# An encoder block on one core: high and low parts of Q and K made in the projection, 64-row third score product, attention's first tiles among the projection's last groups

## What is computed

```python
proj = rmsnorm(h) @ w_in            # 2048 x 2048: q 512, k 512, v 512, u 512
# per head (4), two score maps c=0,1 of depth 64 share one value matrix of width 128
sc = einsum('bqhcd,bkhcd->bhcqk', q, k) * 64**-0.5
p  = softmax(sc - slope_h * |qpos - kpos|)
att = (p[c=0] - lam * p[c=1]) @ v   # lam from four vectors of 64
ssm = bi_s5_glu(u)                  # two-way state-space scan and gate
h = h + concat(rmsnorm(att), ssm) @ w_out
y = rmsnorm(h + relu(rmsnorm(h) @ w_mlp1)**2 @ w_mlp2)
```

## Time and profile before

| | us |
|---|---|
| median of three runs | 2686.13 |
| the three runs | 2683.91, 2686.13, 2692.33 |
| span of the profiled execution | 2681.7 |
| TensorE busy | 2562.9 (96%) |
| VectorE busy | 2093.3 (78%) |
| ScalarE busy | 1416.5 (53%) |
| POOL busy | 327.2 (12%) |

### The profile page before, as it was taken

The page is one execution under the profiler, slowest core; times in us unless marked ns, Lnnn a source line. Parts: engine busy times, 40 slices in busy tenths (PEclk is TensorE's granted clock), DMA queues, the critical chain, the costliest instruction groups (busy, mean ns, idle before and its releaser), DMA issues.

```text
span 2681.7 us, 32621 instructions
## 1 busy us (share of the span) xinstructions
PE 2562.9 (96%) x12804; PEld 2155.2 (80%) x12804; DVE 2093.3 (78%) x2074; ACT 1416.5 (53%) x1737; POOL 327.2 (12%) x221
## 2 busy tenths in 40 slices
PE   7998998999999998988989999999999999999998
PEld 5887777999999986766867888888887888888886
DVE  5866638999999976776898877677888886678885
ACT  3276616878787772224444566543334665543334
POOL 6310001101010003320334000000014000000003
PEclk8999998999999999998999999999999999999999
DMA  5356643020204008977565554452234664452221
GB/s 182 111 181 224 221 135 79 25 69 23 72 23 109 24 11 227 267 232 271 186 220 219 220 222 173 173 219 95 94 111 160 247 219 173 173 204 94 94 79 63
DMA packets 162520, 397.17 MB, mean 148 GB/s; under 512 B 29376, under 2 KB 86976, under 8 KB 134592
## 3 DMA queue, kind: packets, MB, share of 16 engines
q1 hardware_dynamic: 145664, 319.06, 35.9%
q10 hardware_dynamic: 16704, 76.03, 7.2%
HBM read 270.79 MB, written 122.16 MB: 147 GB/s over the span
## 4 chain that ended last, share of the span: by engine, by line
PE 44%; DVE 3%; POOL 1%; DMA 1%; issue 1%; ACT 0%; DVEq 0%; SPq 0%; ACTq 0%; POOLq 0%
PE ml_bank L2447 15%; PE ml_bank L2449 15%; PE ml_bank L2448 15%; POOL kp_tabs L2056 1%; DMA kp_low<-hn_s 1%; DVE ml_res L2327 0%; DVE ml_hb L2361 0%; DVE ml_b_split L2258 0%; DVE ml_w_split L2269 0%; DVE ml_res L2347 0%; DVE ml_rinv L2353 0%; PE ml_bank L2455 0%; DMA ml_hb<-h_s 0%; DMA hn_s<-ml_hb 0%; DVE kp_low L2282 0%
## 5 line engine op out<-in xcount | busy, mean ns | idle before, releaser
L2447 PE MATMUL ml_bank<-ml_b_split,ml_w_split 128*128 128x512 f32 x2016 | 788.8, 391 | 10.1 <-issue 9.8
L2448 PE MATMUL ml_bank<-ml_b_split,ml_w_split 128*128 128x512 f32 x2016 | 785.8, 390 | 0.0
L2449 PE MATMUL ml_bank<-ml_b_split,ml_w_split 128*128 128x512 f32 x2016 | 785.7, 390 | 0.0
L2447 PEld LDWEIGHTS ml_bank<-ml_b_split,ml_w_split 128*128 128x128 f32 x2016 | 379.3, 188 | 93.9 <-issue 14.6
L2448 PEld LDWEIGHTS ml_bank<-ml_b_split,ml_w_split 128*128 128x128 f32 x2016 | 379.6, 188 | 79.7 <-issue 1.2
L2449 PEld LDWEIGHTS ml_bank<-ml_b_split,ml_w_split 128*128 128x128 f32 x2016 | 379.4, 188 | 79.2
L2056 POOL TENSOR_TENSOR kp_tabs<-kp_tabs,ml_square 128x512 f32<-128x512 f32 x55 | 144.2, 2622 | 1266.4 <-ACT ml_square L2160 1259.9
L942 ACT ACTIVATE at_e<-at_e,at_neg_top 128x2048 f32<-128x2048 f32 x128 | 256.5, 2004 | 43.8 <-DVE at_neg_top L1027 43.8
L1148 PEld LDWEIGHTS at_pv<-at_v,at_a_t 128*128 128x128 f32 x2048 | 258.3, 192 | 16.4
L2327 DVE TENSOR_TENSOR ml_res<-ml_bank,ml_res 128x2048 f32<-128x2048 f32 x75 | 171.5, 2287 | 118.8 <-PE ml_bank L2449 118.8
L2094 ACT ACTIVATE ml_b_split<-kp_u_t 128x2048 fp32r<-128x2048 f32 x54 | 103.5, 1917 | 298.1 <-PE ml_bank L2449 298.1
(11 more groups left out here) (225 smaller groups left out, 4097.9 us busy)
## 6 DMA issues: line engine op xcount, KB each, us to landing
act_s<-ml_res ACTq DMA_DIRECT2D x32, 1024.0 KB, 4.0
kp_wide<-in_w_stream SPq DMA_DIRECT2D x18, 1024.0 KB, 5.1
kp_bp<-in_w_stream SPq DMA_DIRECT2D x18, 1024.0 KB, 5.5
kp_tabs<-in_w_stream SPq DMA_DIRECT2D x18, 1024.0 KB, 5.9
ml_r<-in_w_stream SPq DMA_DIRECT2D x18, 1024.0 KB, 6.7
tab_s<-kp_tabs ACTq DMA_DIRECT2D x32, 512.0 KB, 2.7
kp_low<-hn_s SPq DMA_DIRECT2D x16, 1024.0 KB, 5.5
kp_u_t<-hn_s SPq DMA_DIRECT2D x16, 1024.0 KB, 4.9
```

What stands on the lines that cost most here:

```text
L2447: pe.matmul(out, w_hi[:, w], b_hi[:, b], start=fresh and kt == 0, stop=False, skip_group_check=True)
L2448: pe.matmul(out, w_hi[:, w], b_lo[:, b], start=False, stop=False, skip_group_check=True)
L2449: last = pe.matmul(out, w_lo[:, w], b_hi[:, b], start=False, stop=kt == 3, skip_group_check=True)
```

## The change

Q and K are split where they are evacuated, in projection. VectorE scales the group into qku_out as before, ScalarE copies the high part into v_out (keep_high), VectorE subtracts in place (keep_low), and SyncE stores both, into hi_s and lo_s. Attention has its tiles in memory that the projection has finished with (regions), so that both stages are one block without a barrier. load_q writes high and low straight into q_hl: for c = 0 the high part lies in the upper 64 partitions and the low part in the other, for c = 1 the reverse; load_k brings k_hi twice and k_lo once (c = 0 in the upper 64 partitions, c = 1 in the other). The third product is then 64 rows high. The score buffer alternates with c; the combination is done in two halves; tiles 0 and 1 are scored between the projection's last four groups, and the bias, identity and lambda are made before.

```diff
@@ phase_project, SyncE
-                    sp.dma_start(qk_s[g, :, t], qku_out[:, i % 2]).then_inc(qku_stored[i % 2], 16)
+                sp.wait_ge(hi_ready, i + 1)
+                sp.dma_start(hi_s[g, :, t], v_out[:, i % 2]).then_inc(qku_stored[i % 2], 16)
+                sp.wait_ge(lo_ready, i + 1)
+                sp.dma_start(lo_s[g, :, t], qku_out[:, i % 2]).then_inc(qku_stored[i % 2], 16)
...
             if n == NG - 7:
...
+                attention.load_k(sp, 0)
+                sp.wait_ge(prep.outer_stored, 16 * 2 * NQU)
+                for tile in range(2):
+                    attention.load_q(sp, tile)
+            if n == NG - 3:
...
+                attention.load_v(sp, 0)
@@ phase_project, ScalarE
+        def keep_high(n):
+            act.wait_ge(qku_evacuated, n + 1)
+            stored(act, n)
+            act.activation(v_out[:, n % 2].bitcast(F32R), qku_out[:, n % 2], ACT.Copy).then_inc(hi_ready, 1)
...
         def evacuate_v(n):
...
+            if i < 2:
+                act.wait_ge(qku_stored[i % 2], 32 * SECOND // 2)
@@ phase_project, VectorE
+        def keep_low(n):
+            dve.wait_ge(hi_ready, n + 1)
+            dve.tensor_tensor(qku_out[:, n % 2], qku_out[:, n % 2], v_out[:, n % 2], ALU.subtract).then_inc(lo_ready, 1)
...
             prepare(n)
+            if n < SECOND:
+                keep_low(n)
+            if n == NG - 6:
+                attention.biases(dve)
+                attention.lambda_exponents(dve)
+            if n == NG - 5:
+                attention.lambda_difference(dve)
+            if n == NG - 4:
+                attention.add_bias(dve, 0, 0, 0)
+                attention.add_bias(dve, 0, 0, 1)
+            if n == NG - 3:
+                attention.second_half(dve, 0)
+            if n == NG - 2:
+                attention.first_half(dve, 1)
+            if n == NG - 1:
+                attention.second_half(dve, 1)
+                attention.combine(dve, 0, 1)
@@ phase_project, TensorE
             group(n)
+            if n == NG - 4:
+                for before in range(NG - 6, NG - 4):
+                    evacuated(pe, before)
+                pe.wait_ge(rms_ready, NTB)
+            if n >= NG - 4:
+                attention.scores(pe, (n - NG + 4) // 2, n % 2)
@@ Attention
+    def load_q(self, sp, n):
+        h, s = n // self.NQ, n % self.NQ
+        self.wait(sp, self.scores_done, 4 * (n - 1))
+        for c in range(2):
+            rows = slice(c * DH, (c + 1) * DH)
+            other = slice((1 - c) * DH, (2 - c) * DH)
+            for dst, src in ((rows, self.hi_s), (other, self.lo_s)):
+                sp.dma_start(self.q_hl[dst, n % 2, c].bitcast(F32), src[h, rows, s * P:(s + 1) * P])\
+                    .then_inc(self.q_loaded[n % 2], 16)
...
+    def scores(self, pe, n, half):
...
+        for c in range(2):
+            self.wait(pe, self.biased, 4 * n + 2 * half + c - 1)
+            for bank, keys in enumerate(cols):
+                pe.matmul(self.score[:, c, bank * TB:(bank + 1) * TB], self.q_hl[:, n % 2, c], self.k_hi[h % 2][:, c, keys],
+                          start=True, stop=False)
+        for bank, keys in enumerate(cols):
+            for c in range(2):
+                rows = slice(c * DH, (c + 1) * DH)
+                last = pe.matmul(self.score[:, c, bank * TB:(bank + 1) * TB], self.q_hl[rows, n % 2, c],
+                                 self.k_lo[h % 2][rows, keys], start=False, stop=True)
+                if bank == len(cols) - 1:
+                    last.then_inc(self.scores_done, 1)
@@ phase_attention, SyncE: for n in range(NS)
+            if n + 2 < NS:
+                a.load_q(sp, n + 2)
...
+            if n == NS - NQ + 3:
+                sp.wait_ge(a.pv_done, NS - NQ)
+                head.load(sp)
@@ phase_attention, ScalarE: for n in range(NS + 3)
+            a.copy_turned(act, n - 2, (0, 1))
+            a.exponential(act, n - 1, 1)
+            a.copy_turned(act, n - 2, (2, 3))
+            a.copy_result(act, n - 3)
+            a.exponential(act, n, 0)
@@ phase_attention, VectorE: for n in range(2, NS)
+            a.first_half(dve, n)
+            a.second_half(dve, n)
+            a.combine(dve, n - 1, 1)
@@ phase_attention, TensorE: for n in range(2, NS)
+            a.scores(pe, n, 0)
+            for j in range(2, 4):
+                a.turn(pe, n - 2, j)
+            for j in range(2):
+                a.values(pe, n - 2, j)
+            a.scores(pe, n, 1)
+            for j in range(2, 4):
+                a.values(pe, n - 2, j)
+            for j in range(2):
+                a.turn(pe, n - 1, j)
```

More of the change, by code:

```diff
@@ new lines, in stored, with fresh_x, x_freed @@
+    def stored(eng, i):
+        first = min(i, SECOND) // 2
+        wait(eng, qku_stored[i % 2], 32 * first + 16 * (i // 2 - first))
+    def fresh_x(b):
+        return b > 0 and BLOCK_X[b] != BLOCK_X[b - 1]
+    def x_freed(eng, b, k):
+        freed = sum(fresh_x(c) for c in range(b))
+        if k < KD - 1:
+            eng.wait_ge(x_used, freed * (KD - 1) + k + 1)
+        else:
+            eng.wait_ge(group_done, b * NGROUP)
+    w_pieces = w_in.rearrange("(k p) n -> p k n", p=P)
+    x_tiles = x_t.rearrange("(k p) t -> p k t", p=P)
@@ L779, in phase_attention @@
+    return block, attention
+class Attention:
     NQ = S // P
@@ new lines, in second_half, with biases @@
+    def second_half(self, dve, n):
+        for c in range(2):
+            self.add_bias(dve, n, 1, c)
+            self.negate_top(dve, n, c)
+    def biases(self, dve):
+        for i, (first, count) in enumerate(((self.CENTER, S), (0, self.CENTER))):
+            dve.wait_ge(self.distance_ready, i + 1)
+            distance = self.distance_of(first, count)
+            dve.scalar_tensor_tensor(self.bias[:, first:first + count], distance, -1.0, distance, ALU.mult, ALU.min)\
+                .then_inc(self.bias_ready, 1)
+        dve.wait_ge(self.bias_ready, 2)
@@ new lines, in turn, with values @@
+    def turn(self, pe, n, j):
+        if not 0 <= n < self.NS:
+            return
+        if j % 2 == 0:
+            pe.wait_ge(self.combined, 2 * n + j // 2 + 1)
+        self.wait(pe, self.turned_out, 4 * n + j - 1)
+        for i in range(4):
+            kt = 4 * j + i
+            last = pe.transpose(self.turned[:, j % 2, i * P:(i + 1) * P], self.e[:, n % 2, 0, kt * P:(kt + 1) * P], self.ident[:])
+        last.then_inc(self.turned_done, 1)
+    def values(self, pe, n, j):
+        if not 0 <= n < self.NS:
+            return
+        h = n // self.NQ
+        if j == 0:
+            self.wait(pe, self.pv_out, n - 1)
+            if n % self.NQ == 0:
+                pe.wait_ge(self.v_loaded, 16 * (h + 1))
+        pe.wait_ge(self.turned_out, 4 * n + j + 1)
+        for kt in range(4 * j, 4 * j + 4):
+            last = pe.matmul(self.pv[:, n % 2, 0:P], self.a_t[:, n % 2, kt], self.v[h % 2][:, kt], start=(kt == 0),
+                             stop=(kt == self.NQ - 1))
+        if j == 3:
+            last.then_inc(self.pv_done, 1)
```

1258 lines of the change are left out of this document (578 added, 680 removed).

## The result

The changed kernel takes 2722.96 us (median of four runs, 2719.18 to 2723.25), the kernel before 2689.23 in the same comparison: a ratio of 1.0133, 95% interval 1.0115 to 1.0151. By the ratio it is 36 us slower (the two medians differ by 33.7); 2650 was forecast, 36 faster. The profiled execution has a span of 2721.1 against 2681.7, 39.4 more.

What follows compares the result with a forecast made beforehand. TensorE was taken to bound attention's tile at 9.01 us, VectorE 0.65 us behind. Tiles -37, join -20, projection +8 and Q's lead +13 gave -36 us: 2681.7 - 36 + 4.4 = 2650 us, range 2622 to 2680.

Steps and rivals of the forecast that it cites:

- The join: Between projection and attention: scoring tiles 0 and 1 among projection's last groups starts tile 2 earlier, 20 us gained.
- the state-space stage: Stage after attention: it finds its tiles as before, long before attention ends; change forecast 0.
- What projection pays: Projection: 32 more ScalarE copies and 32 more VectorE subtractions for splitting Q and K cost 8 us, bounds 0 to 16.
- six banks of slack: Projection: most of the added splitting work lies beside matmuls, which have six banks of slack.
- Score products: Attention's tiles: half-height score matmuls run in pairs, so the period falls from 9.01 to 8.4 us, 37 us gained.
- 0.10: Score products: cost in us of each change of array height, four a tile, taken from a state-space change of columns.
- The sum of 8.80: Attention: TensorE's tile in us if half-height pairs run one after the other, 2 x 1.91 + 4.98.
- Rival B: Attention: the array empties fully at each switch, period 8.65 us, tiles gain 22 in place of 37: 2665 us, chance 0.15.
- Rival C: Attention: the half-height matmuls don't overlap, period 8.86 us, tiles gain 9: 2678 us, chance 0.11.
- D: Rival, attention: half-height weight loads aren't hidden, a score block takes 2.56 us, 68 us lost: 2755 us, chance 0.07.
- Q's shorter lead: Attention near tile 54: Q, loaded later than before, queues behind the next stage's loads; 13 us lost once.
- The doubled traffic: Projection: storing high and low parts doubles store traffic, 32 x 256 KB, on a queue with room; costs nothing.

Runs made afterwards that it cites:

- e13: Changed kernel without VectorE's low part of Q and K, ScalarE's high part kept: ratio 1.0070 to the kernel before; projection 18.7 us behind e2.
- e14: Changed kernel without ScalarE's high part of Q and K, VectorE's subtraction kept: ratio 1.0077 to the kernel before; projection 23.3 us behind e2.
- e12: Changed kernel with the splitting given to different engines by projection block, plus the edits of e4 and e8: 2677.99 us, ratio 0.9972 to the kernel before.
- e4: Changed kernel with the next stage's 15 loads spread over tiles 51 to 56, behind each tile's Q loads: ratio 1.0093 to the kernel before.
- e1: Changed kernel with the third score product at full height, 128 rows, in place of half-height pairs: 2730.73 us, ratio 1.0181 to the kernel before.
- e5: Changed kernel with each score block's two pairs of half products run twice, no further switch of height: ratio 1.0341 to the kernel before.
- e8: Changed kernel with lambda, K and the first Q loads issued a group earlier and tile 2's Q before the last group's store: ratio 1.0093 to the kernel before.
- e2: Changed kernel without the high and low parts of Q and K, the evacuated tile stored twice: ratio 1.0000 to the kernel before.
- e11: Changed kernel with the high part on VectorE and the low part on GpSimd, plus the edits of e4 and e8: ratio 1.0007 to the kernel before.

## Why the prediction was wrong

The profiled span grew by 39.4 where the sum said -36, 75 us apart. Two terms hold most of it: the cost in projection, 34 us too small, and the gain of the score products, some 29 too large. The join adds 11 and the state-space stage 5; the tiles' end and Q's lead give back 3. Neither of the two alone gives the sign: with only projection wrong, -36 + 34 is -2, no change; with only the score products wrong, -7. One stage's cost and another stage's gain failed together.

**What projection pays: the largest miss.** Forecast 8, bounds 0 to 16; measured 41.8. The places were right in the main (blocks 1, 2 and 5; block 3's 2.91 was not named), the size was not: about 3 forecast at block 2 and 4 more at block 5, 5.07 and 21.42 measured. I charged an instruction's duration and one wait behind it, and called the rest hidden by six banks of slack. Three things were missing. A high part before ScalarE's other work ties that work to VectorE's evacuation (e13: 18.7). The subtraction was taken at the 0.65 us of the earlier trace rows; the 32 have a mean of 0.98, because of the nine that meet GpSimd's squares, and VectorE was near full already, 45.5 of 50 us busy from 80 to 130 us before the change (e14: 23.3). And I took a block's lag as forgotten at its end. How much of it the next block inherits was not measured; e12 shows only that it isn't all.

The trace of before had the warning about GpSimd, 4 us behind the earlier trace rows: the same subtraction twice, beside GpSimd's own share of K. Beside the earlier trace rows GpSimd only writes (at_e, L910, from 402.17 us); here it reads K:

```profile
406.73 2.46 DVE L1065 TENSOR_TENSOR at_k_lo<-kp_low,at_k_hi 128x512 fp32r<-128x512 f32 x2
406.94 5.86 POOL L919 TENSOR_TENSOR at_k_lo<-kp_low,at_k_hi 128x512 fp32r<-128x512 f32 x4
```

2.46 us for two in place of 1.29; one of them takes 1.76.

**Score products.** Forecast 0.6 a tile, 37 in all; measured 0.11, 7 us over 62 tiles (62 x (9.01 - 8.90)). From tile 2's start to tile 63's, e4, which has no stall for Q there, takes 546.8 us for 555.1 in the kernel before, 8.3 less. Three errors, in order of size. A switch costs 0.19, not 0.10 (e1 and e5): 0.36 a tile. The sum of 8.80 for the new order with no packing supposed that a block of eight costs 1.91 and all else stays; e1 measures 9.05, so grouping the products saved nothing: 0.25. Against that, nothing was lost to other engines, for which I had allowed 0.12. By these 8.28 + 0.36 + 0.25 = 8.89, the measured 8.90; the sum has to close, since the price of a switch was worked out from that period, and the separate evidence for it is the longer blocks under e1 and e5. Rival B had the mechanism with too low a price (0.16), and its period of 8.65 missed the 0.25 as well. Rival C is refuted: e5's pairs cost 0.23, not twice that. D is too: a block stays under 1.9.

**The row that misled.** The 0.10 of the earlier trace rows is a change of columns, read from the gap before the next instruction alone. This switch is also paid before it (1.11 for 1.01) and behind it, and a gap between two starts can't show that; a whole period can.

**The join.** Forecast 20, measured 9.4; with e8's loads 20.8. The way of reckoning was right, and I charged 2 us for the loads of K and the first Q. I didn't look for tile 2's Q: it was issued at 455.30 behind the last group's store (452.24), for whose landing SyncE waits too, and TensorE waited 5.69 us for it, then ran at half clock.

**Q's shorter lead.** Forecast 13; the stall is 10.07 us and with its half clock e4 took back 11.9. Right in place, cause and size.

**The side costs taken for nothing.** The doubled traffic: at most 4 (e2), fair. VectorE's and ScalarE's cover in the tile held, by e5: 0.91 us more work for TensorE made the period 0.91 longer. The state-space stage took 5.2 us more, which I had at 0. In one profiled execution of each variant it takes between 245.7 (e4) and 251.5 us (e11), with no order that follows the edits; what sets it stays open.

## What to carry to other kernels

An instruction added to an engine's program costs its wait too, and all that stands behind it in that engine's order now waits for the producer as well; before calling it hidden, ask what that engine was running ahead with. Packing two half-height matmuls pays well only if several pairs stand together for each switch: here one pair saves 0.23 us and one switch costs 0.19. Moving work to an idle GpSimd isn't free for a VectorE that is full. A duration read from a trace holds for the company that the instruction had there: look at what the other engines were doing beside it. And add up the misses before naming a culprit: here no single one turned the sign.

## What was not expected of the hardware

A pair of 64-row matmuls in opposite halves costs 0.23 us, as one of 128 rows; a change of height costs 0.19 (the mean of down and back), a part of it before the change and a part behind the next operation's start. VectorE's subtraction of two SBUF operands takes 0.68 to 0.70 us, or 1.41 to 1.83 when it starts while GpSimd works, and the excess is GpSimd's remaining time less 0.13 or 0.14; its evacuations from the banks keep 0.68 to 0.69.
